# A decoder layer on one core: sums of squares on GpSimd, two PSUM banks in the sample chunk, and the near bias of the prompt attention added by VectorE

## The reference

```python
x = x + 0.5 * swiglu_ffn(x, norm_ffn1, w_ffn1_in, w_ffn1_out)          # d_ff 2816
z, xbc, dt_raw, q, kc, vc, ks, vs, kw, vw, g_logit = project_mix(x, norm_mix, w_in)
y_ssd = ssd_branch(...)       # Mamba-2 scan, 8 heads of 64, state 128, one state per sample sequence
o_nsa = nsa_fn(...)           # 8 query heads, 2 key heads, head dim 64
x = x + concat(y_ssd, rmsnorm(o_nsa)) @ w_out
x = x + mem_attend(x, mem_kv, norm_mem_q, w_mem_q, w_mem_out)          # 256 memory tokens, 4 heads
x = x + 0.5 * swiglu_ffn(x, norm_ffn2, w_ffn2_in, w_ffn2_out)
y = rmsnorm(x, norm_final)

def rmsnorm(x, g): return x * rsqrt(mean(x * x, -1) + EPS) * g
h = h * chunk_decay + states                                            # step of the scan
# attention of one block of 128 queries, three branches:
logit_c = q . kc * scale + rel_bias_2d(rel_bias, dist_c)                # compressed keys, 63 blocks
logit_s = q . k_sel * scale + bias_s                                    # selected key blocks
logit_w = q . kw * scale + rel_bias_2d(rel_bias, dist_w)                # window of 512 keys
```

## Time and profile before

| | |
|---|---|
| time, median of 3 runs | 2892.91 us (2892.55 to 2894.13) |
| the profiled execution's own time | 2890.69 us |
| its span in the profile | 2889.0 us |
| PE busy | 2669.1 us (92%) |
| VectorE busy | 1585.3 us (55%) |
| ScalarE busy | 1003.5 us (35%) |
| GpSimd busy | 132.0 us (5%) |
| mean granted clock of TensorE | 0.949 of full speed |

### The profile page before, as it was taken

How to read it: one execution, slowest core, us unless ns; L and a number is a source line. 1 busy time by engine, 2 the same in 40 slices (tenths; PEclk the granted TensorE clock), 3 DMA queues, 4 the chain that set the end, 5 groups by cost and what they waited for, 6 DMA issues and landing times. The chain is left out here.

```text
span 2889.0 us, 47283 instructions
## 1 busy us (share of the span) xinstructions
PE 2669.1 (92%) x18982; PEld 2503.6 (87%) x18982; DVE 1585.3 (55%) x2908; ACT 1003.5 (35%) x2116; POOL 132.0 (5%) x174
## 2 busy tenths in 40 slices
PE   6999999999979998999589997797779999999998
PEld 6999999999969997898467774597669999999997
DVE  7767666544164111343467663575586676665334
ACT  6333333311144222221266662344453333332111
POOL 0000000000000000110200003131200000000000
PEclk9999999999989998998599997798989999999999
DMA  3222222412035324130300005303012222242111
GB/s 100 81 73 79 79 72 79 181 76 76 1 138 108 40 75 168 39 102 5 102 23 23 9 1 191 120 11 105 16 41 85 69 79 79 72 146 92 76 75 62
DMA packets 121995, 220.29 MB, mean 76 GB/s; under 512 B 12834, under 2 KB 76754, under 8 KB 120242
## 3 DMA queue, kind: packets, MB, share of 16 engines
q1 hardware_dynamic: 115922, 201.51, 21.8%
q10 hardware_dynamic: 2880, 9.07, 0.8%
q0 software_dynamic: 2976, 6.68, 0.7%
HBM read 170.80 MB, written 48.24 MB: 76 GB/s over the span
## 5 line engine op out<-in xcount | busy, mean ns | idle before, releaser
L659 PE MATMUL ffn_gate_up<-ffn_h_hi,ffn_w 128*128 128x272 f32 x1912 | 559.8, 293 | 48.0 <-DVE ffn_w L816 32.8
L661 PE MATMUL ffn_gate_up<-ffn_h_hi,ffn_w 128*128 128x272 f32 x1912 | 556.7, 291 | 0.0
L660 PE MATMUL ffn_gate_up<-ffn_h_lo,ffn_w 128*128 128x272 f32 x1912 | 554.0, 290 | 0.0
L659 PEld LDWEIGHTS ffn_gate_up<-ffn_h_hi,ffn_w 128*128 128x128 f32 x1912 | 363.3, 190 | 52.1 <-DVE ffn_w L816 20.4
L660 PEld LDWEIGHTS ffn_gate_up<-ffn_h_lo,ffn_w 128*128 128x128 f32 x1912 | 364.1, 190 | 0.0
L661 PEld LDWEIGHTS ffn_gate_up<-ffn_h_hi,ffn_w 128*128 128x128 f32 x1912 | 363.2, 190 | 0.0
L1018 DVE SCALAR_TENSOR_TENSOR x<-ffn_down,x 128x364 f32<-128x364 f32 (+1 forms) x240 | 126.3, 534 | 329.5 <-PE ffn_down L235 329.5
L816 DVE TENSOR_TENSOR ffn_w<-ffn_w_raw,ffn_w 128x512 fp32r<-128x512 f32 x264 | 181.1, 687 | 96.9 <-ACT ffn_w L525 96.7
L525 ACT ACTIVATE ffn_w<-ffn_w_raw 128x512 fp32r<-128x512 f32 x264 | 159.8, 624 | 90.7 <-PE ffn_down L661 76.4
L233 PE MATMUL mix_ps<-h_mix_hi,mix_w_hi 128*128 128x364 f32 x480 | 161.6, 337 | 9.7 <-issue 6.3
L659 PE MATMUL ffn_down<-ffn_h_hi,ffn_w 128*128 128x272 f32 x552 | 163.3, 296 | 7.2 <-DVE ffn_w L816 5.9
(11 more groups left out here) (518 smaller groups left out, 6442.9 us busy)
## 6 DMA issues: line engine op xcount, KB each, us to landing
ffn_w_raw<-in_w_ffn_in SPq DMA_DIRECT2D x88, 512.0 KB, 3.9
scratch_ffn_act<-ffn_prod SPq DMA_DIRECT2D x88, 272.0 KB, 2.6
ffn_h_raw<-scratch_ffn_act SPq DMA_DIRECT2D x44, 544.0 KB, 6.5
mix_w_raw<-in_w_mix SPq DMA_DIRECT2D x20, 512.0 KB, 3.5
ffn_h_raw<-in_w_ffn_out SPq DMA_DIRECT2D x16, 512.0 KB, 9.0
ssd_pages<-in_cmp_pages SPq DMA_DIRECT2D x64, 128.0 KB, 2.1
ffn_w_sum<-in_w_ffn_out SPq DMA_DIRECT2D x14, 512.0 KB, 10.7
scratch_x<-x SPq DMA_DIRECT2D x1, 4368.0 KB, 16.5
```

The lines of the kernel that those rows point to most:

```text
L659: pe.matmul(out, hi, x_hi, start=start, stop=False, skip_group_check=chained)
L660: pe.matmul(out, hi, x_lo, start=False, stop=False, skip_group_check=chained)
L661: mm = pe.matmul(out, lo, x_hi, start=False, stop=stop, skip_group_check=chained)
```

## The change

Four separate edits are made.

1. In the last chunk of both down projections GpSimd adds the first seven squares of a token group (`add_up`, six additions), and PE multiplies ones by that sum and by the eighth square, two sums per group in place of eight. A square waits for the buffer by `added` or `summed`.
2. In the sample chunk the sequences take two PSUM banks in turn (`seq_bank`), PE waits for the state of b-2 where it waited for b-1, and VectorE makes two masks and two decays ahead.
3. In the prompt attention the near bias stays one fp32 table in SBUF, and VectorE adds it to the scores in PSUM ahead of the maximum (waiting for its own addition by `near_added`). The identity matmuls of L2232, the table's rounding and its splitting are gone. Where a unit has five key tiles, the oldest is put last, so that the two near tiles lie side by side in one bank. From query tile 4 on, that oldest key tile and the compressed keys of a window unit are one operand of 192 columns, copied together by GpSimd (`edge_keys`, four copies per query tile), so that the matmuls of L2239 and L2240 are made by those of the key tile.
4. In the tail PE makes scores(0) of the memory attention between the two row tiles of queries(2), and VectorE takes maxima(0) and scale(0) ahead of keep_q(2).

x is also given a second name of type fp32r, which takes no instruction. The diff, without declarations:

```diff
 class RunningSquares:
-    def __init__(self, core, bank, ones, squares):
-        self.core, self.bank, self.ones, self.sq = core, bank, ones, squares
-        self.sq_ready, self.summed = map(core.sem, ("run_sq_ready", "run_summed"))
+    def __init__(self, core, bank, ones, squares, sums):
+        self.core, self.bank, self.ones, self.sq, self.sums = core, bank, ones, squares, sums
+        self.sq_ready, self.added, self.summed = map(core.sem, ("run_sq_ready", "run_sq_added", "run_summed"))
+        self.adds = KT - 2
     def square(self, act, d, x):
         if d >= len(self.sq):
-            act.wait_ge(self.summed, d - len(self.sq) + 1)
+            g, k = divmod(d - len(self.sq), KT)
+            if k == KT - 1:
+                act.wait_ge(self.summed, g + 1)
+            else:
+                act.wait_ge(self.added, self.adds * g + max(k, 1))
         act.activation(self.sq[d % len(self.sq)], x, ACT.Square).then_inc(self.sq_ready, 1)
-    def sum(self, pe, d, g, start, stop):
-        pe.wait_ge(self.sq_ready, d + 1)
-        pe.matmul(self.bank(g)[:, :TG], self.ones[:], self.sq[d % len(self.sq)], start=start, stop=stop
-                  ).then_inc(self.summed, 1)
+    def add_up(self, pool, g):
+        a = self.sums[g % 2]
+        if g >= 2:
+            pool.wait_ge(self.summed, g - 1)
+        for k in range(1, KT - 1):
+            d = g * KT + k
+            pool.wait_ge(self.sq_ready, d + 1)
+            if k > 1:
+                pool.wait_ge(self.added, self.adds * g + k - 1)
+            pool.tensor_tensor(a, self.sq[(d - 1) % len(self.sq)] if k == 1 else a, self.sq[d % len(self.sq)], ALU.add
+                               ).then_inc(self.added, 1)
+    def sum(self, pe, g):
+        out = self.bank(g)[:, :TG]
+        last = g * KT + KT - 1
+        pe.wait_ge(self.added, self.adds * (g + 1))
+        pe.matmul(out, self.ones[:], self.sums[g % 2], start=True, stop=False)
+        pe.wait_ge(self.sq_ready, last + 1)
+        pe.matmul(out, self.ones[:], self.sq[last % len(self.sq)], start=False, stop=True).then_inc(self.summed, 1)
...
                 if fin is not None:
                     fin.stores(sp)
-            if first_loads is not None:
-                @block.gpsimd
-                def _(pool):
+            @block.gpsimd
+            def _(pool):
+                if first_loads is not None:
                     pool.memset(xT[:, :, HALVES * HALF:], 0.0).then_inc(pads_ready, 1)
+                for g in range(GROUPS):
+                    running.add_up(pool, g)
             def fresh(a):
...
                 def sum_of(n):
                     t, g = down_units[n]
-                    running.sum(pe, n, g, t == 0, t == KT - 1)
+                    if t == KT - 1:
+                        running.sum(pe, g)
                 for c in range(chunks):
                     pe.wait_ge(k_ready, 2 * first_k[c + 1])
...
+        seq_bank = (ys, tp_x)
...
                     else:
                         for b in range(DEC_BATCH):
                             pe.wait_ge(xsb_ready, b + 1)
-                            if b:
-                                pe.wait_ge(s_state_ready, b)
+                            if b >= 2:
+                                pe.wait_ge(s_state_ready, b - 1)
                             for g in range(2):
-                                mm = pe.matmul(ys[:, g * 256:(g + 1) * 256], bn[:T, g * P:(g + 1) * P],
+                                mm = pe.matmul(seq_bank[b % 2][:, g * 256:(g + 1) * 256], bn[:T, g * P:(g + 1) * P],
                                                xsb[b % 2][:, 4 * g:4 * g + 4, :], start=True, stop=True)
                             mm.then_inc(st_ready, 1)
                             for j in sample_unit(b):
...
                     else:
                         dve.wait_ge(xs_ready, S + 1)
-                        for b in range(DEC_BATCH):
+                        def mask(b):
                             if b >= 2:
                                 dve.wait_ge(st_ready, S + b - 1)
                             dve.tensor_scalar(xsb[b % 2], xs[:SAMPLE, :].rearrange("p (h d) -> p h d", h=H), core.seq_mask[:SAMPLE, b:b + 1],
                                               None, ALU.mult).then_inc(xsb_ready, 1)
+                        def decay(b):
                             h3 = s_state[b].rearrange("p (h d) -> p h d", h=H)
                             end = b * DEC_SEQ + DEC_SEQ - 1
                             dve.tensor_tensor(h3, h3, grow[:, :, end:end + 1].to_broadcast([P, H, HD]),
                                               ALU.mult).then_inc(s_decayed, 1)
+                        for b in range(2):
+                            mask(b)
+                        for b in range(2):
+                            decay(b)
+                        for b in range(DEC_BATCH):
                             dve.wait_ge(s_decayed, b + 1)
                             dve.wait_ge(st_ready, S + b + 1)
-                            dve.tensor_tensor(s_state[b], s_state[b], ys[:], ALU.add).then_inc(s_state_ready, 1)
+                            dve.tensor_tensor(s_state[b], s_state[b], seq_bank[b % 2][:], ALU.add
+                                              ).then_inc(s_state_ready, 1)
+                            if b + 2 < DEC_BATCH:
+                                mask(b + 2)
+                                decay(b + 2)
...
+        EDGE = P + N_CHUNK
+        edge_keys = spare_r[:, half:half + 2 * 2 * KV_GROUPS * EDGE].rearrange(
+            "p (n a g c) -> p n a g c", n=2, a=2, g=KV_GROUPS)
+        edge_tiles = WINDOW // P
...
-            return range(max(0, i - WINDOW // P) if b else 0, i + 1)
+            kt = list(range(max(0, i - WINDOW // P) if b else 0, i + 1))
+            return kt[1:] + kt[:1] if len(kt) == WINDOW // P + 1 else kt
...
-        near_pair = lambda v: (near_raw[:, :, v], by_pairs(near_hi)[:, :, v], by_pairs(near_lo)[:, :, v])
-        NEAR0, EYE, CMPB, KC, WIN, NEAR1 = range(6)
-        tables = [(*near_pair(0), near_landed[0], 32), (core.ident, eye[:], None, None, 0),
+        EYE, CMPB, KC, WIN = range(4)
+        tables = [(core.ident, eye[:], None, None, 0),
-                  (win_raw, win[:], None, win_landed, 16), (*near_pair(1), near_landed[1], 32)]
-        split_count = {NEAR0: 1, CMPB: 2, KC: 3, NEAR1: 4}
+                  (win_raw, win[:], None, win_landed, 16)]
+        split_count = {CMPB: 1, KC: 2}
...
+                pool.wait_ge(split_done, split_count[KC])
+                pool.wait_ge(hi_done, WIN + 1)
+                for i in range(edge_tiles, tiles):
+                    pool.wait_ge(k_ready[1], (i - edge_tiles) // 2 + 1)
+                    if i >= edge_tiles + 2:
+                        pool.wait_ge(s_ready, per_tile * (i - 1))
+                    first = (i - edge_tiles) * P
+                    for a, (keys, blocks) in enumerate(((k_hi, kc_hi), (k_lo, kc_lo))):
+                        pool.tensor_copy(edge_keys[:, i % 2, a, :, 0:P],
+                                         keys[:, 1, :].rearrange("p (g t) -> p g t", g=KV_GROUPS)[:, :, first:first + P]
+                                         ).then_inc(edge_ready, 1)
+                        pool.tensor_copy(edge_keys[:, i % 2, a, :, P:EDGE], blocks[:]).then_inc(edge_ready, 1)
+                    edge = b == 1 and i >= edge_tiles
...
-                    if u == 0:
-                        pe.wait_ge(split_done, split_count[NEAR0])
+                    if u == 1:
                         pe.wait_ge(hi_done, EYE + 1)
-                    if u == 1:
                         pe.wait_ge(split_done, split_count[KC])
                     if u == SET:
-                        pe.wait_ge(split_done, split_count[NEAR1])
                         pe.wait_ge(hi_done, len(tables))
                     if u >= 2:
                         pe.wait_ge(p_ready, u - 1)
+                    if edge and u % per_tile == 1:
+                        pe.wait_ge(edge_ready, 4 * (i - edge_tiles + 1))
                     for c in range(0, len(kt), 4):
                         part = kt[c:c + 4]
                         bank = s_ps[:, s + c // 4, :]
                         keys = slice(g * SEQ + part[0] * P, g * SEQ + (part[-1] + 1) * P)
-                        pe.matmul(bank[:, 0:len(part) * P], qs, k_hi[:, b, keys], start=True, stop=False)
-                        mm = pe.matmul(bank[:, 0:len(part) * P], qs, k_lo[:, b, keys], start=False, stop=True)
-                        close = [j for j in part if i - j < 2]
-                        if close:
-                            at = bank[:, (close[0] - part[0]) * P:(close[-1] - part[0] + 1) * P]
-                            cols = slice((1 - i + close[0]) * P, (2 - i + close[-1]) * P)
-                            for table in (near_hi, near_lo):
-                                mm = pe.matmul(at, eye[:], table[:, h, cols], start=False, stop=True,
```

(36 more changed lines are left out.)

32 lines of the change are left out of this document (15 added, 17 removed).

## The result

The changed kernel takes 2860.1 us (median of 4 runs, 2857.8 to 2860.3) where the kernel before takes 2892.7 in the same comparison (2890.4 to 2894.1). The ratio is 0.9886, with a 95% interval of 0.9869 to 0.9903. It is 33 us faster; 58 were forecast, and 2860 lies outside the range of 2820 to 2855.

The account below looks back on a forecast made before the run. PE was taken as the bound in the FFN chunks and prompt attention, no engine in the sample chunk. -20.2 - 10.5 - 28.7 + 1.3 = -58.1 us from 2890.69 gives 2832.6, median 2835, range 2820 to 2855.

Parts of the forecast that it names:

- the 3.3 at which they would have shown: FFN down projections: GpSimd additions of 3.3 us, three times the assumed 1.11, would outlast a unit and shrink the gain.
- the mix nearer the full clock: Sample chunk: last add ends at 1390.4, between 1389.5 at full and 1392.8 at half clock, giving -10.5 us.
- a clock of 0.5 in tiles 1 to 3: Prompt attention: listed among the signs that would make the prediction wrong.
- a chain between engines longer than either's own work: Listed sign of error: scores, addition, maximum, exponential and the bank free again two units on outlast either engine's work.
- the length stays at about 101: Prompt attention tiles 1 to 3: VectorE at 97.0 us becomes the bound, with 4 us of waits; 0 us (-3 to +8).
- The clock was a rival at 7%: Prompt attention tiles 1 to 3: the clock falls and matmuls cost twice; one tile gives 2855 us; chance 0.07.
- 79% is above the 70% of the row at full clock: Argument against a falling clock: PE busy about 79 of 101 us in tiles 1 to 3, against 2.79 of 4.
- +20 us for a fallen tile: Prompt attention tiles 1 to 3: a tile with 27 us of PE work becomes 53 where it lasted 34.
- I give PE 6 us of waits where it had 3: Prompt attention tiles 4 to 7: PE 161.0 and VectorE 158.3 are level, so 167.0 for 190.7, -23.7 us.
- VectorE paces the whole: Prompt attention: an addition at 0.70 us makes edit 3 give -7 or so, total 2857; at 0.58, 2848; chance 0.16.
- Tile 0, -5 us: Prompt attention tile 0: PE loses 16 x 0.34 = 5.4 us at half clock; -5 us, range -6 to 0.

Follow-up runs that it names:

- The bias left out: The changed kernel without VectorE's addition, so the near bias is missing from the result; 2845.3 us (one run).
- the filler: Two more 256-column matmuls per unit in query tiles 0 to 3: 2860.48 us on the changed kernel, 2842.6 (one run) with the near bias also left out.

## Why the prediction was wrong

**Edit 1** was right: -19.5 us measured, -20.2 forecast, with units 2.50 us apart and additions (0.96 us) far from the 3.3 at which they would have shown. **Edit 2** was right: -10.7 for -10.5, at VectorE's pace but for the last add, the mix nearer the full clock that was forecast. **Edit 4** was right: +1.2 for +1.3.

**Edit 3** carries the whole miss, +0.8 for -28.7, and three steps of it failed. The prediction had named both causes among what would make it wrong: a clock of 0.5 in tiles 1 to 3, and a chain between engines longer than either's own work.

*Tiles 1 to 3, "the length stays at about 101"* (by the cuts of the earlier trace rows): they grew by 15.0 us. The bias left out shows that 8.6 of it need no work of VectorE at all, and the filler takes 6.7 of those away again; that part is the granted clock. The rest, 111.8 - 105.5 = 6.3 us, came with the addition. The clock was a rival at 7%, dismissed by "79% is above the 70% of the row at full clock". That compared a mean over three tiles with one stretch of 4 us. Like with like, the kernel before has PE busy 23.3 of 28.0 us in tile 1 (83%), and after the change the same work less 3.8 us would be some 19.5 us in 28 to 30, 65 to 70%. The mean over tiles 1 to 3 hid the thinnest one. The row also came from a stretch in which the clock was already up, and what failed in tile 1 is that it rose late. The rule of the Trainium skill that was named there ("TensorE: Matmul & The Clock Gate", "A second HAM failure mode: psum-queue depth-cycling") speaks of a clock that goes to and fro between its two levels where PE idles briefly between groups of matmuls. The traces agree in tiles 2 and 3, at mean clocks of 0.90 and 0.96 with one fall each; in tile 1, at 0.55, the clock mostly stayed down. At +20 us for a fallen tile the price was too high by far: tile 1 grew by 8.8 us. It was worked out for the mean tile, with 27 us of PE work, and tile 1 has less; at half clock its 32 us of PE work still fit beside VectorE's 27.

*Tiles 4 to 7, "I give PE 6 us of waits where it had 3"*: they gave 11.5 us, not 23.7. Both engines' work came out nearly as summed (PE 164.3 for 161.0, VectorE 155.9 for 158.3), but the waits are 17.5 us on PE and 25.9 on VectorE. PE's work fell by 26.1 us and its waits for VectorE's scaled probabilities rose from 2.7 to 16.8, at 16 places of 64 units, 13 of them behind a copy: that is the difference. Each total left VectorE room; single units did not, and with at most about a unit between the engines, room in one unit did not help another. That the whole length is the sum over units of the slower step fits these numbers but was not worked out unit by unit. The rival "VectorE paces the whole" had this stretch's -11 by luck: it took a dearer addition (0.70) and VectorE as the bound throughout, where at 0.414 it held PE up at these places only.

*Tile 0, -5 us*: it gave 1.5. PE lost 5.5 us of work and VectorE gained 4.9; VectorE's idle time fell by 6.5 and PE's rose by 4.0: PE's wait for the compressed keys ahead of unit 1 grew from 4.4 to 6.1 us and its waits for scaled probabilities from 1.2 to 5.3. The prediction knew of the first wait and still counted the saving of all 16 units, the one ahead of it too, and it gave the tile hardly any further waits. Even with the bias left out the tile took 32.6 us.

That 2860 lies only 5 us outside the range says little: with tiles 1 to 3 at their old length the time would have been some 2845, inside it, with half the gain of tiles 4 to 7 still missing.

Not foreseen: the -2.9 us between FFN 1's end and the sample chunk. The mixed projection's first 48 us run at changing clocks (0.78 and 0.80 before, 0.57 and 0.92 after), and kernels with the same instructions there differ by up to 5.5 us in this stretch, so nothing in it is laid to the change; what moves it stays open.

## What to carry to other kernels

Work moved off a full engine is not won where a hand-over ties it to the engine that receives it; where the two stand nearly level, look at the units in which the receiver has most to do (here those with a copy), not at each engine's total. Before taking matmuls from a stretch at full clock, look at where the clock rises and at PE's gaps in its thinnest part, and not at a mean over the stretch; the clock can cost more than the matmuls did. And split an edit that does several things: the part that only removed PE work (the operand of 192 columns, one near pair) matched the whole gain of tiles 4 to 7 by itself, as long as VectorE made its copies.

## What the runs showed of the hardware

More matmuls can take less time: with the filler (594 matmul records in three tiles for 498) tiles 1 to 3 went from 105.5 to 98.8 us, because the granted clock of tile 1 went from 0.50 to 0.83 and of tiles 2 and 3 from 0.87 to 1.00. The rise of the clock is not fixed by the instructions: with the same ones in tile 1 its mean clock was 0.98 in one kernel and 0.89 and 0.84 in two others. A 256-column addition by VectorE in PSUM with an SBUF operand takes 0.43 us, and one of 128 columns 0.29; GpSimd's addition of 128x364 in SBUF took 0.97 us beside the down projection, where the tail's, in the earlier trace rows, takes 1.11.
